# The factors of o: from a diagonal and a product to two transfers through memory

## The chip, the cores and the metric

The kernel runs on one core of a Trainium2 chip. The metric is the device time of one execution in microseconds. TensorE (PE in the profile) multiplies, VectorE (DVE), ScalarE (ACT) and GpSimd (POOL) work elementwise, SyncE (SP) issues most of the transfers.

## The reference, cut to what matters

A trunk of four layers over 528 tokens (16 meta tokens and 512 of the input) of 1024 channels: a mixer and a gated feed-forward block in each. The second mixer is a differential attention with 8 heads, and only it is touched:

```
s = q k^T * scale + bias                      # two score maps (c = 0, 1) per head
p = softmax(where(mask, s, -inf))
wts = p[:, :, 0] - lam * p[:, :, 1]
o = wts @ v                                   # 128 channels per head
o = rmsnorm(o, subln_g, 1e-5) * (1 - lam_init)
return o.reshape(B, L, 1024) @ w_o
```

The rmsnorm is over the 128 channels of one head, so each head has one factor 1/rms for each of the 528 tokens, and o is multiplied by it.

## The kernel before, in words

Each matrix product is done in three: every operand is split in a high part (rounded, type fp32r) and a low part (the rest), and hi x hi, lo x hi and hi x lo are summed. ACT makes high parts, DVE low parts.

In the attention o lies with the channels of a head on the 128 partitions and the tokens along the free dimension (`o_raw`, 128x528). The factor of a token must therefore be known on every partition. It comes about like this for head h:

- ACT copies the product of weights and v from PSUM to `o_raw` and squares it into `o_sq` (`copy_rows`, L1797 on). PE sums the squares over the partitions (`o_sums`, L1333), which puts token sums in five columns of 128 partitions, that is token j*128+p on partition p, column j, and the meta tokens in the fifth.
- DVE adds the epsilon and makes a first guess of the root (`guess_factors`, L2421 on, `rsqrt_seed`, L1987). It also tells POOL by the semaphore `o_guessed`.
- POOL refines the guess in two steps on 128x5 numbers (`row_factors`, L775 to L793), then scales the identity by each of the five columns into a diagonal `o_diag` of 128x528 (L796, L797), in the buffer that is called `square` in the profile.
- PE multiplies a matrix of ones by the diagonal (`spread_factors`, L1336 on, L1343 and L1344): each partition of PSUM banks 7 and 6 then holds all 528 factors.
- DVE multiplies `o_raw` by them and by the gain (`norm_rows`, L2440 and L2442) and drains. ACT makes the high part of o (`o_hi`, L1819) and DVE the low part (`o_lo`, L2450) in the next step, as operands of the output projection.

The work is a software pipeline whose order is written out by hand: each engine has its own `attention_step` (PE L1391 on, ACT L1821 on, DVE L2460 on), and step h does the q, k and v projection of head h, the scores, softmax and weights of head h-1, and the o of head h-2. Each engine runs its list in order, and semaphores tie them. Step 0 only projects, step 1 has no older head, steps 2 to 7 do all three, step 8 projects nothing (PE fills in with the output projection), and step 9 does the o of the last head, for which DVE and ACT build the diagonal by themselves. PE and DVE run steps 4 to 7 as a hardware loop, POOL ran its seven steps as one.

In one step of PE: half of the q projection between the transposes of the older head's last weights (L1309, L1385), weights times v (L1322), then score blocks 0 to 4 (L1298; block j is 128 queries against 16+(j+1)*128 keys, block 4 is the 16 meta queries) set between pieces of the k and v projection (L856), and turned weights. All score blocks use PSUM bank 4 and 5, so block j waits for the maxima of block j-1 (`scores_read`, L1298's `wait`). On DVE: for each block `row_maxima` (adds the bias, takes the maxima, L2378 and L2384), on ACT `exponentials` (L1780), on DVE `combine` (L2393 to L2398, the weights of a block), and `weights_lo` for the low part of the turned weights (L2412 to L2417). `norm_rows` of the older head stands on DVE between `row_maxima` of block 3 and `combine` of block 3, and `spread_factors` on PE in the third part of the v projection before score block 4. PSUM banks 6 and 7 are shared in turn by six users per step (last weights, v, sums, first weights, o's factors, third weights), which `turn_number` numbers: PE counts `turned`, and the readers count `turned_lo` when a bank may be overwritten.

Of the kernel before, what the change touches and what calls it, by code (L numbers as in the profile page):

```python
# [26 lines left out]
F32 = mybir.dt.float32  # L27
F32R = mybir.dt.float32r
I32 = mybir.dt.int32
ALU = mybir.AluOpType  # L30
ACT = mybir.ActivationFunctionType
ds = bass.ds

P = 128
# [146 lines left out]
class Memory:  # L181


    def __init__(self, nc, ctx):
# [93 lines left out]
        self.o_diag = self.square  # L278
        row_maxima = new("row_maxima", [P, 8])
# [41 lines left out]
class Semaphores:  # L321


    def __init__(self, sem):
# [64 lines left out]
        self.o_diagonal = sem("o_diagonal")  # L389
        self.o_rooted = sem("o_rooted")  # L390
# [66 lines left out]
def turn_number(h, what):  # L457

    if isinstance(h, int) and h == 1:
        return {"v": 0, "w01": 1, "w2": 2}[what]
    if isinstance(h, int) and h == HEADS + 1:
        return 6 * h - 9 + {"w3": 0, "sums": 1, "o": 2}[what]
    return h * 6 + ({"w3": 0, "v": 1, "sums": 2, "w01": 3, "o": 4, "w2": 5}[what] - 9)
# [27 lines left out]
def trunk(nc, a, out):  # L495
# [3 lines left out]
    with ctx:  # L499
# [5 lines left out]
        rel_once = nc.dram_tensor("rel_once", [HEADS, REL_PITCH], F32, kind="Internal").ap()  # L505
        bands_dram = nc.dram_tensor("bands_scratch", [P, 4, BANDS], F32, kind="Internal").ap()
# [187 lines left out]
        def _(pool):  # L694
# [80 lines left out]
            def row_factors(hd):  # L775
# [19 lines left out]
                for j in range(QT):  # L795
                    pool.tensor_scalar(m.o_diag[:, j * P:(j + 1) * P], m.ident[:, :], m.o_r[:, j:j + 1], None, ALU.mult)  # L796
                pool.tensor_scalar(m.o_diag[0:META, QT * P:TOK], m.ident[0:META, 0:META], m.o_r[0:META, QT:QT + 1],  # L797
                                   None, ALU.mult).then_inc(s.o_diagonal, 1)


            with pool.Fori(1, HEADS) as hd:
                pool.wait_ge(s.scores_read, hd * 5)
                pool.tensor_copy(m.bias_cur[:, :], m.bias[:, ds(hd * TOK, TOK)]).then_inc(s.bias_cur_ready, 1)
# [46 lines left out]
        def _(pe):  # L850
# [485 lines left out]
            def spread_factors(h):  # L1336

                pe.wait_ge(s.o_diagonal, h + 1)
                parts = ((0, DVE_TILES), (DVE_TILES, QT)) if isinstance(h, int) and h == HEADS - 1 else ((0, QT),)
                for n, (j0, j1) in enumerate(parts):  # L1340
# [46 lines left out]
            def attention_step(h, par, proj, mid, old):  # L1387
# [54 lines left out]
                if old:  # L1442
                    banks67_free(h, "o")
                    spread_factors(h2)
# [10 lines left out]
            def attention_end():  # L1455
# [17 lines left out]
                spread_factors(h2)  # L1473
# [493 lines left out]
        def _(dve):  # L1967
# [453 lines left out]
            def guess_factors(h, step):  # L2421
# [4 lines left out]
                if isinstance(h, int) and h == HEADS - 1:  # L2426
                    dve.wait_ge(s.o_diagonal, h)
# [9 lines left out]
            def norm_rows(h, step):  # L2437

                dve.wait_ge(s.turned, turn_number(step, "o") + 1)
# [249 lines left out]
```

## Time and profile before

| what | value |
|---|---|
| time, median of 3 runs | 2067.81 us (2063.7 to 2068.21) |
| profiled execution, span from the first to the last instruction | 2061.8 us |
| busy share of the span: PE, DVE, ACT, POOL | 98%, 76%, 43%, 11% |
| mean granted clock of TensorE | 0.987 |
| median of the runs over the profiled span | 6.0 us |

No time of its own is given for the profiled execution beside its span; what lies around the span is only known as the distance to the timed runs. A row of a timeline has the start in us from the beginning of the span, the duration in us, the engine, the line, the operation, what it writes and reads, the sizes, the count of merged instructions, and in brackets the idle time before and what ended it. Ends of matrix products are modelled, so their starts are the better numbers.

### The profile page before, as it was taken

How to read it: one execution, taken by the hardware profiler on the slowest of the kernel's cores; microseconds unless marked ns; L12 is line 12 of the kernel's file. 1: busy time of each engine (PE TensorE's matmuls, PEld its weight loads, DVE VectorE, ACT ScalarE, POOL GpSimd, SP SyncE). 2: the span in 40 equal slices, each digit the busy share in tenths (PEclk: the TensorE clock that was granted, in tenths of full speed). 3: DMA queues.
4: the chain of work that ended last, by engine and by line, in shares of the span. 5: the costliest groups of instructions: out<-in, count | busy, mean ns of one | idle time of the engine just before them, and what ended most of it. 6: DMA issues, size and time to landing. Idle time of an engine off the chain costs nothing.

```text
span 2061.8 us, 40642 instructions
## 1 busy us (share of the span) xinstructions
PE 2020.2 (98%) x16006; PEld 1950.4 (95%) x16006; DVE 1572.3 (76%) x2265; ACT 877.4 (43%) x1364; POOL 236.1 (11%) x340
## 2 busy tenths in 40 slices
PE   7999999999998999999999999999999999999998
PEld 7999999988887999999999999999999988999997
DVE  6797788766776579778877886687787867977794
ACT  6443334334444334333438764343343434433342
POOL 5000000412122400000041111100000061000000
PEclk9999999999998999999999998999999999999999
DMA  5423333331121132333336641233433422233332
GB/s 164 135 83 102 102 102 98 90 112 53 51 61 51 52 92 83 102 102 102 98 102 135 138 108 42 72 93 93 122 100 83 119 77 82 82 102 102 102 103 93
DMA packets 305226, 195.14 MB, mean 95 GB/s; under 512 B 7034, under 2 KB 297851, under 8 KB 304852
## 3 DMA queue, kind: packets, MB, share of 16 engines
q1 hardware_dynamic: 299932, 175.08, 29.6%
q0 software_dynamic: 3984, 14.08, 3.2%
q10 hardware_dynamic: 1192, 4.34, 0.5%
q8 instruction: 82, 1.34, 0.3%
q14 instruction: 36, 0.29, 0.0%
HBM read 179.44 MB, written 6.44 MB: 90 GB/s over the span
## 4 chain that ended last, share of the span: by engine, by line
PE 85%; DVE 6%; issue 3%; POOLq 1%; DVEq 1%; ACT 1%; DMA 1%; SPq 0%; POOL 0%; ACTq 0%
PE ps L856 42%; PE ps L1120 31%; PE ps L973 2%; PE ps L1231 2%; PE ps L914 1%; PE ps L1322 1%; PE ps L1298 1%; DVE w_lo L1974 1%; PE ps L957 1%; DVE w_lo L2213 1%; POOLq L750 1%; DVEq L2249 1%; DVEq L2218 1%; POOLq L747 1%; PE ps L883 1%
## 5 line engine op out<-in xcount | busy, mean ns | idle before, releaser
L1120 PE MATMUL ps<-t_lo,y_hi 128*128 128x264 f32 (+1 forms) x1008 | 285.7, 283 | 0.0
L1120 PE MATMUL ps<-t_lo,w_hi 128*128 128x264 f32 (+1 forms) x1008 | 285.7, 283 | 0.0
L1120 PE MATMUL ps<-t_hi,w_lo 128*128 128x264 f32 (+1 forms) x1008 | 285.5, 283 | 0.0
L1120 PE MATMUL ps<-t_hi,y_lo 128*128 128x264 f32 (+1 forms) x1008 | 285.3, 283 | 0.0
L1120 PE MATMUL ps<-t_hi,w_hi 128*128 128x264 f32 (+1 forms) x1008 | 285.1, 283 | 0.1
L1120 PE MATMUL ps<-t_hi,y_hi 128*128 128x264 f32 (+1 forms) x1008 | 284.8, 283 | 0.0
L1685 ACT ACTIVATE w_hi<-w_raw 128x1024 fp32r<-128x1024 f32 (+1 forms) x108 | 127.8, 1201 | 329.4 <-PE ps L856 193.8
L856 PE MATMUL ps<-hid_hi,w_hi 128*128 128x264 f32 (+1 forms) x1184 | 265.3, 296 | 1.6 <-DVE hid_lo L2269 1.6
L856 PE MATMUL ps<-hid_lo,w_hi 128*128 128x264 f32 (+1 forms) x1184 | 264.6, 296 | 0.0
L856 PE MATMUL ps<-hid_hi,w_lo 128*128 128x264 f32 (+1 forms) x1184 | 264.1, 295 | 0.0
L856 PE MATMUL ps<-y_hi,w_hi 128*128 128x264 f32 (+1 forms) x1088 | 244.1, 301 | 4.3 <-POOLq L827 2.3
L856 PE MATMUL ps<-y_lo,w_hi 128*128 128x264 f32 (+1 forms) x1088 | 234.6, 292 | 0.0
L856 PE MATMUL ps<-y_hi,w_lo 128*128 128x264 f32 (+1 forms) x1088 | 234.3, 292 | 0.0
L1685 ACT ACTIVATE y_hi<-w_raw 128x1024 fp32r<-128x1024 f32 (+1 forms) x108 | 125.8, 1197 | 166.2 <-DVE w_raw L2223 134.3
L856 PEld LDWEIGHTS ps<-hid_hi,w_hi 128*128 128x128 f32 x1184 | 187.2, 188 | 7.8 <-DVE hid_lo L2269 2.2
L856 PEld LDWEIGHTS ps<-hid_lo,w_hi 128*128 128x128 f32 x1184 | 187.6, 188 | 5.5
L856 PEld LDWEIGHTS ps<-hid_hi,w_lo 128*128 128x128 f32 x1184 | 187.4, 188 | 5.7
L1120 PEld LDWEIGHTS ps<-t_hi,w_hi 128*128 128x128 f32 x1008 | 189.8, 188 | 0.7 <-DVE h L2309 0.5
L1120 PEld LDWEIGHTS ps<-t_hi,y_hi 128*128 128x128 f32 x1008 | 189.8, 188 | 0.0
L1120 PEld LDWEIGHTS ps<-t_lo,w_hi 128*128 128x128 f32 x1008 | 189.5, 188 | 0.1
L1120 PEld LDWEIGHTS ps<-t_hi,w_lo 128*128 128x128 f32 x1008 | 189.5, 188 | 0.0
L1120 PEld LDWEIGHTS ps<-t_hi,y_lo 128*128 128x128 f32 x1008 | 189.5, 188 | 0.0
(317 smaller groups left out, 4410.9 us busy)
## 6 DMA issues: line engine op xcount, KB each, us to landing
w_raw<-in_ffn_w_gate SPq DMA_DIRECT2D x88, 512.0 KB, 5.0
w_raw<-in_ffn_w_up SPq DMA_DIRECT2D x88, 512.0 KB, 4.6
w_raw<-in_ffn_w_down SPq DMA_DIRECT2D x70, 512.0 KB, 4.3
w_raw<-in_ffn_w_down SPq DMA_DIRECT2D x24, 384.0 KB, 4.3
w_raw<-in_attn_w_qkv SPq DMA_DIRECT2D x16, 512.0 KB, 3.7
w_raw<-in_conv_w_in SPq DMA_DIRECT2D x16, 512.0 KB, 4.2
w_lo<-w_raw POOLq DMA_DIRECT2D x16, 512.0 KB, 5.4
w_raw<-in_attn_w_qkv SPq DMA_DIRECT2D x16, 256.0 KB, 2.9
```

The costliest lines, as they stand in the source:

```text
L747: pool.drain()
L750: pool.drain()
L856: mm = pe.matmul(ps[:, bank + hf, 0:half], w[:, slot, col:col + P], x(hf), start=begin and w is m.w_hi and n == 0, stop=end and w is m.w_lo)
L883: mm = pe.matmul(ps[:, 7, at:at + 1], blk(square, d, t, P), m.ones[:, 0:1], start=True, stop=True)
L914: mm = pe.matmul(out, y[:, at:at + rows], w[:, (t0 + g) % SLOTS, k * 256:(k + 1) * 256], start=k == 0 and n == 0, stop=k == 1 and n == 2)
L957: mm = pe.matmul(out[:, c0:c1], z, m.bands[0:TILE_ROWS[i], g, at:at + c1 - c0], start=i == 2 and n == 0, stop=i in (1, 4) and n == 1)
L973: mm = pe.matmul(ps[:, 4 * par + 2 + r, 0:cols_n], w[rows, par, :, :].rearrange("p t c -> p (t c)")[:, pairs_of_taps], u[rows, par, (j - r ...
L1120: mm = pe.matmul(ps[:, bank, 0:hw], w[:, at:at + P], b[:, t, k, 0:hw], start=k == 0 and n == 0, stop=k == 3 and n == 2)
L1231: mm = pe.matmul(bank, x, w, start=False, stop=k == LAST_F - 1 and n == 2)
L1298: mm = pe.matmul(ps[:, (4, proj_banks(par, 1))[part] + c, col:col + k1 - k0], q[rows, q0:q0 + P], k[rows, k0:k1], start=n == 0, stop=n == 2)
L1322: pe.matmul(ps[:, 4, q0:QT * P], v[0:rows, vi, :], w, start=n == 0 and x == 0, stop=n == QT and x == 2)
L1685: act.activation(hi[:, sub * SUB:(sub + n_sub) * SUB], src, ACT.Copy).then_inc(s.op_hi, 1)
```

## The change

For heads 0 to 6 the diagonal and the product with ones are gone. POOL, after its two steps of refinement, writes the 128x5 factors to a row of 640 numbers in memory, token by token, waits for that transfer, and reads the first 528 back to all 128 partitions by a second transfer, into the same buffer that held the diagonal (`o_factors`). Two semaphores, `factors_out` and `factors_in`, count them. The seven POOL steps are now written out instead of looped.

PE issues no spreading for these heads, and the numbering of banks 6 and 7 has five users per step. On DVE `norm_rows` waits for `factors_in`, reads the factors from SBUF, and stands later: behind `row_maxima` of block 4, the reading of v, and the low parts of q and k, before the low part of the third weights. For head 7 everything stays as it was.

```diff
@@ Memory
         self.o_diag = self.square
+        self.o_factors = self.square
@@ turn_number
     if isinstance(h, int) and h == HEADS + 1:
-        return 6 * h - 9 + {"w3": 0, "sums": 1, "o": 2}[what]
-    return h * 6 + ({"w3": 0, "v": 1, "sums": 2, "w01": 3, "o": 4, "w2": 5}[what] - 9)
+        return 5 * h - 7 + {"w3": 0, "sums": 1, "o": 2}[what]
+    return h * 5 + ({"w3": 0, "v": 1, "sums": 2, "w01": 3, "w2": 4}[what] - 7)
@@ POOL
+        factors_dram = nc.dram_tensor("o_factors_scratch", [(QT + 1) * P], F32, kind="Internal").ap()
...
-                for j in range(QT):
-                    pool.tensor_scalar(m.o_diag[:, j * P:(j + 1) * P], m.ident[:, :], m.o_r[:, j:j + 1], None, ALU.mult)
-                pool.tensor_scalar(m.o_diag[0:META, QT * P:TOK], m.ident[0:META, 0:META], m.o_r[0:META, QT:QT + 1],
-                                   None, ALU.mult).then_inc(s.o_diagonal, 1)
-            with pool.Fori(1, HEADS) as hd:
+                wait(pool, s.factors_in, hd * 16)
+                with nc.allow_non_contiguous_dma(reason="one factor a token"):
+                    pool.dma_start(factors_dram.rearrange("(j p) -> p j", p=P), m.o_r[:, :]).then_inc(s.factors_out, 16)
+                pool.wait_ge(s.factors_out, hd * 16 + 16)
+                pool.dma_start(m.o_factors[:, :],
+                               factors_dram[0:TOK].rearrange("(o n) -> o n", o=1).to_broadcast([P, TOK]))\
+                    .then_inc(s.factors_in, 16)
+            for hd in range(1, HEADS):
                 pool.wait_ge(s.scores_read, hd * 5)
-                pool.tensor_copy(m.bias_cur[:, :], m.bias[:, ds(hd * TOK, TOK)]).then_inc(s.bias_cur_ready, 1)
+                pool.tensor_copy(m.bias_cur[:, :], m.bias[:, hd * TOK:(hd + 1) * TOK]).then_inc(s.bias_cur_ready, 1)
                 row_factors(hd - 1)
@@ PE
-            def spread_factors(h):
-                pe.wait_ge(s.o_diagonal, h + 1)
-                parts = ((0, DVE_TILES), (DVE_TILES, QT)) if isinstance(h, int) and h == HEADS - 1 else ((0, QT),)
-                for n, (j0, j1) in enumerate(parts):
+            def spread_last_factors():
+                pe.wait_ge(s.o_diagonal, 1)
+                for n, (j0, j1) in enumerate(((0, DVE_TILES), (DVE_TILES, QT))):
...
                 fill(2, 2, 5)
-                if old:
-                    banks67_free(h, "o")
-                    spread_factors(h2)
                 if mid:
                     score(h1, par, 4)
@@ DVE
             def norm_rows(h, step):
-                dve.wait_ge(s.turned, turn_number(step, "o") + 1)
-                dve.scalar_tensor_tensor(out=m.o_raw[:, META:], in0=ps[:, 7, :], scalar=m.sub_gain[:, 0:1],
+                last = isinstance(h, int) and h == HEADS - 1
+                if last:
+                    dve.wait_ge(s.turned, turn_number(step, "o") + 1)
+                    tokens, meta = ps[:, 7, :], ps[:, 6, 0:META]
+                else:
+                    dve.wait_ge(s.factors_in, h * 16 + 16)
+                    tokens, meta = m.o_factors[:, 0:SEQ], m.o_factors[:, SEQ:TOK]
+                dve.scalar_tensor_tensor(out=m.o_raw[:, META:], in0=tokens, scalar=m.sub_gain[:, 0:1],
...
                     row_maxima(h1, par, 3)
-                if old and mid:
-                    norm_rows(h2, h)
                 if mid:
                     combine(h1, 3)
                     row_maxima(h1, par, 4)
...
                         dve.tensor_tensor(lo[:, :], x[:, :], hi[:, :].bitcast(F32), ALU.subtract)\
                            .then_inc(s.qk_ready, 1)
+                if old and mid:
+                    norm_rows(h2, h)
                 if mid:
                     weights_lo(h, "w2", 2, 2)
                     combine(h1, 4)
```

## Rows read from the trace of the kernel before

**Rows 1.** The page: busy time and share of the engines, and the chain by engine.
```profile
PE 2020.2 (98%) x16006; PEld 1950.4 (95%) x16006; DVE 1572.3 (76%) x2265; ACT 877.4 (43%) x1364; POOL 236.1 (11%) x340
...
PE 85%; DVE 6%; issue 3%; POOLq 1%; DVEq 1%; ACT 1%; DMA 1%; SPq 0%; POOL 0%; ACTq 0%
```

**Rows 2.** Timeline of PE in step 4 (start, duration, engine, line, operation, tiles, count).
```profile
533.96 0.45 PE L1298 MATMUL ps<-k_hi,q_hi 64*128 64x400 f32 x2
...
541.60 1.02 PE L1343 MATMUL ps<-square,ones 128*128 128x512 f32 x2
...
542.87 0.28 PE L1298 MATMUL ps<-k_hi,q_hi 64*128 64x16 f32 x2
...
549.17 0.65 PE L1309 MATMUL ps<-ident,weights 128*128 128x128 f32 x4
...
549.88 0.33 PE L1385 MATMUL ps<-ident,weights_meta 128*128 128x128 f32 x1
...
553.88 0.49 PE L1322 MATMUL ps<-wtm_hi,v_hi 16*128 16x512 f32 x1
```

**Rows 3.** Timeline of DVE in step 4.
```profile
542.59 0.17 DVE L2384 TENSOR_SCALAR row_maxima<-row_maxima 128x2 f32<-128x2 f32 x1
542.98 0.75 DVE L2440 SCALAR_TENSOR_TENSOR o_raw<-ps,lam_s,o_raw 128x512 f32<-128x512 f32 x1 [0.22 <-PE ps L1344]
543.65 0.23 DVE L2442 SCALAR_TENSOR_TENSOR o_raw<-ps,lam_s,o_raw 128x16 f32<-128x16 f32 x1
544.38 0.16 DVE L2393 RECIPROCAL row_maxima<-row_sums 128x1 f32<-128x1 f32 x1 [0.50 <-ACT scores L1780]
...
548.38 0.55 DVE L2412 TENSOR_TENSOR wt_lo<-ps,wt_hi 128x384 fp32r<-128x384 f32 x1
...
549.60 0.22 DVE L2398 SCALAR_TENSOR_TENSOR weights_meta<-scores,row_maxima 16x16 f32<-16x16 f32 x1
```

**Rows 4.** Timeline of PE in step 1, which has no older head.
```profile
443.65 0.45 PE L1298 MATMUL ps<-k_hi,q_hi 64*128 64x400 f32 x2
...
452.42 0.28 PE L1298 MATMUL ps<-k_hi,q_hi 64*128 64x16 f32 x2 [0.98 <-DVE row_maxima L2384]
...
458.81 0.65 PE L1309 MATMUL ps<-ident,weights 128*128 128x128 f32 x4 [0.15 <-DVE wtm_lo L2417]
```

**Rows 5.** Timeline of DVE in step 1.
```profile
453.98 0.16 DVE L2393 RECIPROCAL row_maxima<-row_sums 128x1 f32<-128x1 f32 x1 [1.61 <-ACT scores L1780]
```

**Rows 6.** The last refining multiplication, grouped (durations min/median/max in ns).
```profile
L793 POOL TENSOR_TENSOR o_r<-o_t,o_r x14: 195/198/1149, 474.5 to 657.3; 128x5 f32<-128x5 f32 x14
```

**Rows 7.** Timeline of POOL, steps 4 and 8.
```profile
537.54 2.35 POOL L796 TENSOR_SCALAR square<-ident,o_r 128x128 f32<-128x128 f32 x4 [0.17 <-issue]
...
657.67 2.34 POOL L796 TENSOR_SCALAR square<-ident,o_r 128x128 f32<-128x128 f32 x4 [0.17 <-issue]
```

**Rows 8.** Transfers: tiles, issuing queue, count, size of each, median us to landing.
```profile
w_raw<-in_attn_w_qkv SPq DMA_DIRECT2D x16, 256.0 KB, 2.9
...
bias<-rel_scratch POOLq DMA_DIRECT2D x1, 2112.0 KB, 10.0
...
cv_sum<-cv POOLq DMA_DIRECT2D x7, 264.0 KB, 6.7
```

**Rows 9.** Timeline of PE in step 8.
```profile
660.45 2.05 PE L1343 MATMUL ps<-square,ones 128*128 128x512 f32 x2 [2.19 <-POOL square L797]
...
669.48 0.60 PE L1309 MATMUL ps<-ident,weights 128*128 128x128 f32 x4
```

**Rows 10.** Timeline of DVE in step 8.
```profile
662.86 0.17 DVE L2384 TENSOR_SCALAR row_maxima<-row_maxima 128x2 f32<-128x2 f32 x1
...
666.61 0.54 DVE L2412 TENSOR_TENSOR wt_lo<-ps,wt_hi 128x384 fp32r<-128x384 f32 x1
...
668.01 0.22 DVE L2398 SCALAR_TENSOR_TENSOR weights_meta<-scores,row_maxima 16x16 f32<-16x16 f32 x1
```

**Rows 11.** Stretches: PE, PEld, DVE, ACT, POOL busy (instructions), granted clock, DMA share, GB/s.
```profile
658.00:662.00 4.00, 1.81 (x6) 0.50 (x2) 2.96 (x11) 0.62 (x2) 2.31 (x5) 0.50 0.00 0
```

More of the change, by code:

```diff
@@ L389, in __init__ @@
         self.o_diagonal = sem("o_diagonal")
+        self.factors_out = sem("factors_out")
+        self.factors_in = sem("factors_in")
         self.o_rooted = sem("o_rooted")
@@ L1472, in attention_end @@
                 banks67_free(HEADS + 1, "o")
-                spread_factors(h2)
+                spread_last_factors()
                 attn_out(2, HEADS - 2)
@@ L2425, in guess_factors @@
                                          in1=m.row_eps[:, :], op0=ALU.mult, op1=ALU.add).then_inc(s.turned_lo, 1)
-                if isinstance(h, int) and h == HEADS - 1:
-                    dve.wait_ge(s.o_diagonal, h)
                 rsqrt_seed(m.o_x[:, :], m.o_r[:, :]).then_inc(s.o_guessed, 1)
@@ L2437, in norm_rows @@
             def norm_rows(h, step):
-                dve.wait_ge(s.turned, turn_number(step, "o") + 1)
-                dve.scalar_tensor_tensor(out=m.o_raw[:, META:], in0=ps[:, 7, :], scalar=m.sub_gain[:, 0:1],
+                last = isinstance(h, int) and h == HEADS - 1
[6 more added lines that the diff above has]
+                dve.scalar_tensor_tensor(out=m.o_raw[:, META:], in0=tokens, scalar=m.sub_gain[:, 0:1],
                                          in1=m.o_raw[:, META:], op0=ALU.mult, op1=ALU.mult)
-                dve.scalar_tensor_tensor(out=m.o_raw[:, 0:META], in0=ps[:, 6, 0:META], scalar=m.sub_gain[:, 0:1],
-                                         in1=m.o_raw[:, 0:META], op0=ALU.mult, op1=ALU.mult)\
-                   .then_inc(s.turned_lo, 1)
+                e = dve.scalar_tensor_tensor(out=m.o_raw[:, 0:META], in0=meta, scalar=m.sub_gain[:, 0:1],
+                                             in1=m.o_raw[:, 0:META], op0=ALU.mult, op1=ALU.mult)
+                if last:
+                    e.then_inc(s.turned_lo, 1)
                 dve.drain().then_inc(s.o_normed, 1)
```

## The prediction

> **What bounds the kernel now.** First the busy table: PE is busy 98% of the span, DVE 76%, and the chain that ended last is put down to PE for 85% [rows 1]. By these two alone, a PE instruction that goes is time won. But they are averages, and the change touches only one stretch, the attention. So next I read one step of its loop on PE and DVE, and ask of each PE instruction there which wait would end last. I take the step that holds the spreading product at 541.60. Five more look like it (spreading at 481.26, 511.27, 571.84, 602.48 and 632.75); the seventh product stands in the last step, which has no projection.
>
> What the reader is to see on PE [rows 2]: spreading from 541.60 to the fifth score block (64x16) at 542.87; transposes of the last weights at 549.17 and 549.88; weights times v at 553.88. On DVE [rows 3]: the fourth block's maxima are there at 542.59+0.17 = 542.76; the factors are multiplied in from 542.98 to 543.65+0.23 = 543.88; then DVE idles 0.50 us until ACT has the exponentials of that block. From 544.38 on it is nearly without a pause up to the meta rows' weights, 549.60+0.22 = 549.82, and PE transposes exactly those at 549.88. It runs on to the first maxima of the next scores, which PE's product at 553.88 waits for. So PE is full, but at 549.88 DVE is right behind it: the cover is 0.06 us.
>
> **Part 1: the product goes from PE.** It held PE for 542.87-541.60 = 1.27 us. But the next instruction, the fifth score block, writes the banks that the fourth's maxima are read from, and so waits for 542.76. With the spreading gone PE waits there for DVE. The trace holds a control: the loop's first step with scores has neither spreading nor factors, and there PE waited 0.98 us for the row maxima before this very block [rows 4]. From its third score block to the transposes of the last weights that step took 458.81-443.65 = 15.16 us; the step with spreading took 549.17-533.96 = 15.21 [rows 2, 4]. I value the removed product at nothing. Bounds: a gain of 1.2 us per step if no wait takes its place, and 0; a loss is excluded but for the clock (a rival below).
>
> **Part 2: the multiplication moves on DVE.** It leaves the place where DVE waits for ACT anyway: in the control step, which has no multiplication, that wait is 1.61 us instead of 0.50 [rows 3, 5], so what follows is not earlier. It goes behind q_lo and k_lo, into the stretch where DVE has no pause. Behind it stand the low part of the third weights and the meta weights (PE asks for both, at 549.17 and 549.88), the low part of a weight tile, o_lo, the low part of the fourth weights, and the first maxima (PE asks at 553.88). Its size is 543.65-542.98 = 0.67, plus 0.23: 0.90 us [rows 3]. The drain behind it adds a little, the cover of 0.06 takes a little off; I leave both out. PE is dense from there to the next step's third score block, so DVE's lateness is handed on whole and nothing gives it back. Six steps: 6 x 0.90 = 5.4 us. Bounds per step: 0, if something before it has slack that I don't see, and 1.1 with a drain and a wait of 0.1 each way; a gain is excluded, since nothing in front of it gets shorter. The factors are now read from SBUF, not PSUM; that could move its size a few hundredths. ACT's rounding of o follows it; ACT is busy 43% [rows 1] and has time to move it in.
>
> **Part 3: POOL and the two transfers.** POOL's scalings (four of 128x128 in 2.35 us from 537.54 [rows 7], and a small one) go; POOL is idle after them, so nothing by itself. The transfers start instead of them at 537.54, and DVE comes to the multiplication at 548.38 [rows 3]: a cover of 10.8 us. The first writes 640 runs of 4 bytes, the second reads a row of 2112 bytes for each of 128 partitions. The trace shows neither. Nearest rows [rows 8]: 256 KB loaded by SP land in 2.9 us; 264 KB that POOL accumulates in 6.7; POOL's 2112 KB in 1024 runs in 10.0. The second transfer has the size of the first two, the queue of the one and the plain copy of the other: the middle, 4.8. The first has next to no bytes but 640 runs: above 2.9, and far under 10.0, whose bytes alone are eight times 256 KB; I take 4.7, nearer to 2.9. Sum 9.5, there 1.3 us before DVE asks: hidden, at nothing. Bounds: 2 x 2.9 = 5.8 and 10.0+6.7 = 16.7. Between the two POOL waits; behind it in its queue is the copy of the next head's bias, which starts only at 546.66: hidden too. SP's load of a weight tile issued at 537.48 shares the DMA engines; the row of 2.9 us is of such loads and holds them.
>
> One kind of delay is shown: the same small multiplication on POOL took 0.20 us as a median and 1.15 at most [rows 6], so something holds POOL up for 0.95. One such hold per transfer adds 1.9 us, and 9.5 becomes 11.4: late by 0.6. The Trainium skill's page SBUF — State Buffer (SBUF: two separate sides) speaks against the change: a GpSimd-issued transfer has its descriptors written over a port that it shares with VectorE, and can stand while VectorE runs in a 2-port mode, 620 ns becoming 3100. By it (an estimate from the page) two transfers are up to 5 us later, 14.5, and the kernel 6 x 3.7 + 4.7 = 27 us slower still. The row shows the hold, not one of that length.
>
> **Part 4: the last step.** PE's wait of 2.19 us for POOL and the spreading behind it go [rows 9]. But the fifth score block again waits for the maxima, 662.86+0.17 = 663.03 [rows 10], and the spreading had ended about there (two products from 660.45, 2.05 us, and two small ones): nothing gained. DVE comes to the multiplication at 666.61. What PE asks for at 669.48 was ready at 668.01+0.22 = 668.23 [rows 9, 10], so 0.90 fits; the transfers, from 657.67 [rows 7], have 8.9 us and the 0.3 that is left, 9.2. The clock is another matter: the two products of 128x512 took 2.05 us here and 1.02 in the loop [rows 2, 9], and from 658 to 662 the granted clock is 0.50, the lower level of 1.2 GHz, after PE had paused [rows 11]. Without them PE does nothing from 660.45-2.19 = 658.3 to 663.0. If the clock comes back later by the 2.6 us of work that is gone, PE gets 1.3 less done. Bounds 0 and 1.3; I take the middle, 0.7.
>
> **Sum.** 5.4 + 0.7 = 6.1 us slower, against the profiled span of 2061.8: 2067.9. The runs shown (2063.7 to 2068.21) have a median of 2067.81, 6.0 above that span with what lies around it; kept, it gives **2073.9 us**.
>
> **Rivals.**
> Late factors. One mechanism: the pair of transfers takes over 10.8 us, DVE stands, and all that part 2 names stands behind it. From there each microsecond costs one in each of six steps, in the last from 9.2 on. Two of POOL's 6.7 are 13.4: 6 x 2.6 + 4.2 = 20 more, 2094; at 12.3: 6 x 1.5 + 3.1 = 12 more, 2086. For it: POOL's rows and the hold. Against: both transfers are small. Chance 0.27.
>
> PE is the bound; this is the other side. If the fifth block's wait is short and DVE has a microsecond of cover at 549.88, the chain's own count holds: 6 x 1.2 = 7.2 saved, in the last step up to 663.0-658.3 = 4.7: 12 faster, 2056. For it: 98% and 85%. Against: the control's 0.98 us, and the cover of 0.06. Chance 0.10.
>
> Absorbed: DVE's move meets slack, PE gains nothing, or a part of each cancels: 2064 to 2071. Chance 0.12.
>
> Clock: two waits of about a microsecond in each step bring the granted clock down; 4 us at half speed cost 2 per step, 12 more, 2086. Against: the control waited 0.98 at full clock. Chance 0.01.
>
> The forecast keeps 0.50; its own range is 2071 to 2078.
>
> **How the numbers follow.** About 0.2%, 4.1 us, is what a measurement here can tell from no change: slower means above 2071.9, faster under 2063.7. Slower: 0.45 of the forecast, 0.28 of late factors and clock, together 0.73. Same: 0.05 of the forecast, 0.12 absorbed, 0.17. Faster: 0.10. The range goes down to 2065, which leaves out the PE rival, and up to 2087, which leaves out factors later than about 12.4 us, another 0.10.
>
> **What would show it.** In the trace after: PE idle some 1.2 us between the fourth and fifth score block, released by the row maxima; a second wait of PE, of about 1 us, before the transposes of the last weights or the meta weights; from the third score block to those transposes 16.1 us instead of 15.2; DVE's wait for exponentials before the fourth weights over 1 us; no idle time of DVE before the multiplication. If that distance stays at 15.3 or less, part 2 is wrong. If DVE idles before the multiplication, part 3 is, and the length of that wait times six is what the first rival adds.

## The result, and the profile after

The kernel after takes **2108.95 us** (median of 4 runs, 2107.69 to 2113.84), the kernel before 2068.01 on the same chip; the ratio is **1.0222**, 95% interval [1.021, 1.0233]. The prediction of 2073.9 and its range up to 2087 are missed by far; only the direction is right. The profiled execution after spans 2105.8 us, 44.0 more than the 2061.8 of before. (Of all executions below, one of e10's six took 3928.44 us; what disturbed it isn't known, and no ratio uses it.)

The page after, busy table, chain by engine and the two new transfers (the rows that answer to [rows 1] and [rows 8]):

```profile
PE 2025.9 (96%) x15978; PEld 1960.1 (93%) x15978; DVE 1574.3 (75%) x2265; ACT 879.9 (42%) x1364; POOL 227.5 (11%) x319
...
PE 78%; issue 9%; DMA 4%; POOLq 4%; DVE 3%; DVEq 1%; ACT 1%; POOL 0%; SPq 0%; ACTq 0%
...
square<-o_factors_scratch POOLq DMA_DIRECT2D x7, 264.0 KB, 4.4
...
o_factors_scratch<-o_r POOLq DMA_DIRECT2D x7, 2.5 KB, 8.9
```

The last number of a transfer's row is the median time from issue to landing. The smallest transfer of the kernel, 2.5 KB, takes 8.9 us, twice as long as the 264 KB behind it.

PE in step 4, from the third score block to that of the next step (answers to [rows 2]; in brackets the idle time before, and who ended it):

```profile
546.45 0.45 PE L1305 MATMUL ps<-k_hi,q_hi 64*128 64x400 f32 x2
...
555.31 0.28 PE L1305 MATMUL ps<-k_hi,q_hi 64*128 64x16 f32 x2 [1.05 <-DVE row_maxima L2387]
...
567.13 1.12 PE L1316 MATMUL ps<-ident,weights 128*128 128x128 f32 x4 [5.54 <-DVE wtm_lo L2420]
568.25 0.42 PE L1391 MATMUL ps<-ident,weights_meta 128*128 128x128 f32 x1
...
584.16 0.45 PE L1305 MATMUL ps<-k_hi,q_hi 64*128 64x400 f32 x2
```

The removed product has become a wait of 1.05 us for the row maxima, as in the control step of [rows 4]. Then there is a second wait, 5.54 us, before the last weights' transposes. From the third block to them it is now 567.13-546.45 = 20.68 us where it was 15.21. The prediction had 16.1.

DVE and POOL in that step (answers to [rows 3] and [rows 7]):

```profile
556.88 0.16 DVE L2396 RECIPROCAL row_maxima<-row_sums 128x1 f32<-128x1 f32 x1 [1.62 <-ACT scores L1783]
...
560.16 0.69 DVE L2519 TENSOR_TENSOR k_lo<-k,k_hi 128x528 fp32r<-128x528 f32 x1
565.25 0.75 DVE L2447 SCALAR_TENSOR_TENSOR o_raw<-square,lam_s,o_raw 128x512 f32<-128x512 f32 x1 [4.40 <-DMA square<-o_factors_scratch]
565.92 0.23 DVE L2449 SCALAR_TENSOR_TENSOR o_raw<-square,lam_s,o_raw 128x16 f32<-128x16 f32 x1
```
```profile
550.36 0.20 POOL L797 TENSOR_TENSOR o_r<-o_t,o_r 128x5 f32<-128x5 f32 x1
551.13 0.91 POOL L801 DMA_DIRECT2D o_factors_scratch<-o_r  x1 [0.57 <-issue]
560.73 0.59 POOL L803 DMA_DIRECT2D square<-o_factors_scratch  x1 [8.69 <-DMA o_factors_scratch<-o_r]
```

POOL has its factors at 550.56. It takes 0.57 us to get to the first transfer, waits until 560.73 for it, and DVE is released at 565.25: 14.7 us, where DVE was ready after 560.85-550.56 = 10.3. DVE stands for 4.40 us, and the third and meta weights stand behind it. In all it waits 25.2 us over seven steps (us in total, times, longest):

```profile
DVE o_raw L2447 <- DMA square<-o_factors_scratch: 25.2, 7, 5.9
```

What the transfer does in that time is seen in the first two stretches, of 2 us each (PE, PEld, DVE, ACT, POOL busy, granted clock, DMA share, GB/s); the last two rows, of 4 us, show the clock behind PE's long pause, the one before them 40 us of the loop:

```profile
556.00:558.00 2.00, 2.00 (x18) 2.00 (x18) 0.95 (x3) 1.92 (x6) 0.00 (x0) 1.00 0.00 0
558.00:560.00 2.00, 2.00 (x19) 2.00 (x19) 1.73 (x9) 1.23 (x6) 0.00 (x0) 1.00 0.00 0
...
540.00:580.00 40.00, 33.41 (x250) 30.46 (x247) 22.85 (x75) 16.47 (x45) 5.42 (x13) 0.91 0.18 47
...
566.00:570.00 4.00, 2.87 (x14) 2.41 (x15) 3.62 (x11) 1.93 (x5) 0.00 (x0) 0.50 0.00 0
570.00:574.00 4.00, 4.00 (x25) 3.86 (x24) 2.98 (x14) 1.05 (x5) 0.00 (x0) 0.72 0.50 140
```

From 556 to 560 the DMA engines show no busy time at all, though the transfer issued at 551.13 has not landed: it is waiting, not moving. The records of the DMA engines say the same in finer steps: the last of its sixteen packets has ended at 553.65, and its sixteen completions come one by one from 554.54 to 560.43. And behind the pause of 5.54 us the granted clock is at its lower level (0.50, 1.2 GHz), just where PE has work again. From the transposes to the next step's third score block it took 584.16-567.13 = 17.03 us; before it took 564.20-549.17 = 15.03, and e1 below, in the new order and at full clock, takes 15.02. So the clock costs this step 2.0 us more. The whole step lasts 584.16-546.45 = 37.71 us instead of 30.24.

The 44 us lie in the attention alone. Two marks serve for all kernels: the third score block of step 2 (before 473.62, after 472.96) and PE's wait of 1.52 us for o_lo at the end of the last head (before 686.85, after 730.61):

```profile
730.61 0.51 PE L863 MATMUL ps<-o_hi,w_hi 128*128 128x264 f32 x2 [1.52 <-DVE o_lo L2458]
```

Between them lie 213.2 us before and 257.6 after, 44.4 more. I call this distance the stretch. Six steps of the loop take 38.7 of it (third block of step 2 to that of step 8, at 652.62 before and 690.70 after), the last step 5.7. The 38.7 divide in DVE's waits for factors, 25.2 - 5.9 (the last step's) = 19.3; the moved multiplication, some 5.8 (measured below, in e1); and a remainder of 13.6. Step by step against e1, the way from the last weights' transposes to the next third block is 0.6 to 2.8 us longer, 11.3 in the six steps: this is the clock. Of the 2.3 left, 2.0 are DVE instructions that lasted longer beside POOL's copy of the next bias (shown with e3).

### The profile page after: what moved, and what is told of

Read it like the earlier page. It is cut to its first block, busy times and chain, and to the rows that moved or that the text cites. A ratio compares the mean times of both kernels' runs of the same rounds, so it can differ in the third digit from the quotient of the medians.

```text
span 2105.8 us, 40518 instructions
## 1 busy us (share of the span) xinstructions
PE 2025.9 (96%) x15978; PEld 1960.1 (93%) x15978; DVE 1574.3 (75%) x2265; ACT 879.9 (42%) x1364; POOL 227.5 (11%) x319
## 4 chain that ended last, share of the span: by engine, by line
PE 78%; issue 9%; DMA 4%; POOLq 4%; DVE 3%; DVEq 1%; ACT 1%; POOL 0%; SPq 0%; ACTq 0%
PE ps L863 37%; PE ps L1127 33%; DMA o_factors_scratch<-o_r 3%; PE ps L980 2%; PE ps L1238 2%; POOLq L754 1%; PE ps L921 1%; POOLq L751 1%; PE ps L964 1%; PE ps L890 0%; POOLq L796 0%; DVE w_lo L2216 0%; DVEq L2252 0%; PE ps L897 0%; PE ps L877 0%
```

## Experiments

For each kernel the stretch is given against the 213.2 us of before; it is free of the few microseconds by which executions differ ahead of the attention. The kernel before, run again beside the experiments, took 2063.3 to 2064.7 us as a median, less than the 2068.01 above; so kernels are compared by their ratios, and each stretch is that of one execution.

### The parts one by one

**e1_no_transfers** keeps the moved multiplication and takes the transfers out:
```diff
-                [POOL's two transfers and its waits for them]
+                pool.engine_nop().then_inc(s.factors_in, 1)
...
-                    dve.wait_ge(s.factors_in, h * 16 + 16)
+                    dve.wait_ge(s.factors_in, h + 1)
-                    tokens, meta = m.o_factors[:, 0:SEQ], m.o_factors[:, SEQ:TOK]
+                    tokens, meta = m.rstd[:, 0:SEQ], m.rstd[:, SEQ:TOK]
```


> Left out: both transfers; the multiplication takes the row of rstd (already in SBUF) in place of the factors, so o is scaled wrongly; DVE waits only for POOL's last refining step. All else as in the changed kernel. Theory (late transfers cost 25 us of waiting, the falling clock behind them about 12, the moved multiplication 0.97 us in each of six steps, the removed product nothing): 2074 us (2072 to 2077), granted clock back at full in steps 2 to 7, third score block to the last weights' transposes 16.1 us. Rival, PE is the bound and its product was worth 1.2 us a step: 2056 to 2062. Rival, the move itself brings the clock down and costs most: above 2085.

**e2_old_place** is e1 with `norm_rows` back between the maxima of block 3 and the weights of block 3:
```diff
                     row_maxima(h1, par, 3)
+                if old and mid:
+                    norm_rows(h2, h)
                 if mid:
                     combine(h1, 3)
```


> As e1 (no transfers, the multiplication takes rstd), but the multiplication stands at its old place, before the weights of the fourth block. What is left of the change is that PE has no spreading product. Theory: the fifth score block waits about 1.0 us for the row maxima instead, so 2068 us as before, within 2, third score block to last transposes 15.2 us. Rival, PE is the bound: 7 x 1.2 and 2 to 4 more in the last step gained, 2056 to 2060.

Measured: e1 2072.19 us, ratio 1.0048 [1.0032, 1.0065], stretch +5.6. e2 2064.18, ratio 1.0005 [0.9995, 1.0015], stretch -1.2. PE in step 4 of e1, then of e2:

```profile
539.38 0.45 PE L1299 MATMUL ps<-k_hi,q_hi 64*128 64x400 f32 x2
...
555.57 0.66 PE L1310 MATMUL ps<-ident,weights 128*128 128x128 f32 x4 [1.08 <-DVE wtm_lo L2414]
...
570.59 0.45 PE L1299 MATMUL ps<-k_hi,q_hi 64*128 64x400 f32 x2
```
```profile
536.53 0.45 PE L1299 MATMUL ps<-k_hi,q_hi 64*128 64x400 f32 x2
...
545.37 0.28 PE L1299 MATMUL ps<-k_hi,q_hi 64*128 64x16 f32 x2 [1.04 <-DVE row_maxima L2381]
...
551.64 0.66 PE L1310 MATMUL ps<-ident,weights 128*128 128x128 f32 x4
```

e2 takes 15.11 us for the distance that took 15.21 before: the product is gone, a wait of 1.04 us stands in its place, and nothing is won. e1 takes 16.19, 0.98 more than before: the multiplication in its new place costs its full length. Both are what the prediction's parts 1 and 2 say. With the transfers away the granted clock is 0.985 again (before: 0.987), and the loss is the 5.6 us of the stretch, where the forecast's sum was 6.1; by its ratio the kernel would have taken 2078 us beside the 2068 of the result, at the edge of the forecast's own range. All the rest of the loss hangs on the transfers.

**e3_unread** does both transfers as the kernel after, but the multiplication doesn't wait for them (DVE only waits, before it overwrites the factors, until the first transfer of the head before has read them):
```diff
-                    dve.wait_ge(s.factors_in, h * 16 + 16)
-                    tokens, meta = m.o_factors[:, 0:SEQ], m.o_factors[:, SEQ:TOK]
+                    dve.wait_ge(s.o_diagonal, h + 1)
+                    tokens, meta = m.rstd[:, 0:SEQ], m.rstd[:, SEQ:TOK]
...
```


> The changed kernel with both transfers running as they do, but nothing on DVE waits for the second: the multiplication takes rstd at its new place. Theory: the transfers cost only by being late, so the same as e1 within 2 us, 2074. Rival, contention: they slow DVE, the weight loads or POOL's copies, 5 us or more above e1.

Measured: 2075.17 us, ratio 1.007 [1.0053, 1.0087]. Its interval overlaps that of e1, though its median is 3.0 us higher, between the theory's 2 and the rival's 5. So the presence of the transfers is worth 0 to some 5 us, and it is the wait for them that costs most. Its stretch is +10.9, 5.3 more than e1's, and the trace shows where they come from. First, POOL copies the next head's bias behind the second transfer, and so later than in e1. In e1 this copy ran beside DVE's reading of v from PSUM, which took 0.69 us as before; in e3 it falls in each of the six steps on a DVE instruction whose inputs are in SBUF, and that instruction lasts 0.50 to 0.83 us longer than its like, 3.8 us in all:

```profile
552.55 1.52 DVE L2522 TENSOR_TENSOR k_lo<-k,k_hi 128x528 fp32r<-128x528 f32 x1
```
```profile
552.86 0.64 POOL L811 COPY bias_cur<-bias 128x528 f32<-128x528 f32 x1
```

In e1 `k_lo` took 0.70 us. Second, two steps took 33.4 and 33.1 us among others of 31.5 to 32.0. In the first of the two, PE paused 1.87 us (e1: 1.08), and the clock fell behind it:

```profile
554.00:558.00 4.00, 2.13 (x15) 1.76 (x16) 3.66 (x11) 1.71 (x5) 0.00 (x0) 0.93 0.33 68
558.00:562.00 4.00, 4.00 (x24) 3.86 (x22) 3.17 (x14) 1.26 (x5) 0.00 (x0) 0.65 0.47 131
```

The length of the pause doesn't decide it by itself: in e3 pauses of 1.87 and 1.61 us before these transposes were followed by the lower level, those of 1.57, 1.69, 1.69 and 1.73 us were not; e1 and e4 stayed at 1.00 in the loop with 0.9 to 1.4 us. In the kernel after all six (4.2 to 5.5 us) were followed by it. The clock is thus a second part of the cost, behind the wait.

### What makes the first transfer long

**e4_runs20** writes the five factors of a partition side by side, 128 runs of 20 bytes. The tokens' order in the row is then another, so that o is scaled by other tokens' factors.
```diff
-    pool.dma_start(factors_dram.rearrange("(j p) -> p j", p=P), m.o_r[:, :])
+    pool.dma_start(factors_dram.rearrange("(p j) -> p j", p=P), m.o_r[:, :])
```


> The changed kernel, with the scratch row laid out partition by partition, so that the first transfer writes 128 runs of 20 bytes instead of 640 of 4; the row then comes back in another order, so o is scaled by the wrong tokens' factors. Theory A, the number of runs makes the first transfer long (8.9 us): it falls to 4 to 5 us, DVE waits little or nothing, the clock stays up, 2075 to 2080. Rival B, it is the fixed cost of a transfer issued by POOL that writes to memory: it stays above 8 us and the kernel above 2103.

**e5_runs_doubled** writes 128x10 numbers, 1280 runs of 4 bytes:
```diff
-    pool.dma_start(factors_dram.rearrange("(j p) -> p j", p=P), m.o_r[:, :])
+    pool.dma_start(factors_dram.rearrange("(j p) -> p j", p=P), m.o_r2[:, :])    # 128 x 10
```


> The changed kernel, but the first transfer writes 1280 runs of 4 bytes (the five factors and five ones of each partition) instead of 640; the second reads the same first 528 numbers. Theory, the cost is by the run: from 3.0 us with 128 runs and 8.9 with 640 it is 11.5 ns per run, so 16.3 us now, 7.4 more in each of seven steps: the changed kernel plus 52, and more where PE, idle for longer, gets its clock back later: 2160 to 2180. Rival, a step between 20-byte and 4-byte runs and not their number: first transfer under 10.5 us and under 2120.

Measured: e4 2070.59 us, ratio 1.0039 [1.0025, 1.0054], stretch +5.9, no wait of DVE for factors. e5 2113.19 (2 runs), ratio 1.0233 [1.0213, 1.0254], stretch +48.3. POOL's waits for the first transfer, e4 and e5 (us in total, times, longest; after: 58.6, 7, 9.2):

```profile
POOL square L803 <- DMA o_factors_scratch<-o_r: 19.6, 7, 3.7
```
```profile
POOL square L805 <- DMA o_factors_scratch<-o_r: 66.1, 7, 10.2
```

e4's theory A held (3.0 us, where it said 4 to 5): take the short runs away and the remaining cost is the multiplication's. e5 missed by far. I had divided the 5.9 us between e4 and after by the 512 runs between them, 11.5 ns each, and expected 2160 to 2180. Doubling the runs added 1.1 us per transfer, under 2 ns a run, as its rival had it (under 10.5 us for the transfer, under 2120 for the kernel). The number of runs is not what most of the 8.9 us is made of. In the next three kernels the second transfer reads a row of an input instead of the scratch row, so the factors are other numbers.

**e11_one_column** sends 128 factors only, **e12_spread64** all 640 with 64 bytes from each to the next, **e14_near** all 640, 8 bytes apart, partition by partition. **e6_sp_queue** leaves the transfers as they are and lets SP issue them.
```diff
@@ e11_one_column
+    pool.dma_start(factors_dram[0:P].rearrange("(p j) -> p j", j=1), m.o_r[:, 0:1])
@@ e12_spread64
+    pool.dma_start(factors_dram.rearrange("(j p n) -> p j n", p=P, n=16)[:, :, 0:1], ...m.o_r...)
@@ e14_near
+    pool.dma_start(factors_dram.rearrange("(p j n) -> p j n", p=P, n=2)[:, :, 0:1], ...m.o_r...)
@@ e6_sp_queue
+                sp.wait_ge(s.o_diagonal, hd + 1)
...
+                    sp.dma_start(factors_dram.rearrange("(j p) -> p j", p=P), m.o_r[:, :]).then_inc(s.factors_out, 16)
...
```


> The first transfer sends only the first column of o_r: 128 runs of 4 bytes to 128 neighbouring words, in place of 640; the second transfer reads a row of an input of the same size (left out: the true factors, so o is scaled by other numbers). The kernel after took 8.9 us for 640 runs of 4 bytes, 128 runs of 20 bytes took 3.0 us, 1280 runs of 4 bytes about 10. Theory A, the number of runs up to some hundreds sets it: the first transfer takes about 3 us here, as with 20-byte runs, and the time is near 2070. Theory B, each run under some size makes a slow write whatever their number: it stays at 8 to 9 us, and the time near 2105. Theory C, 4-byte writes that are neighbours in memory wait for each other: between the two, 4 to 7 us, since 128 of them are still neighbours.

> The first transfer sends all 640 factors as 4-byte runs, but each to its own word 64 bytes from the next, so no two share 64 bytes of memory; the second transfer reads a row of an input of the same size (left out: the true factors). Theory A (number of runs): 8.9 us as in the kernel after, time near 2108. Theory B (each short run is a slow write): the same 8.9. Theory C (neighbouring short writes wait for each other): 3 to 4.5 us, and the time falls to 2070 to 2080.

> The first transfer sends all 640 factors as 4-byte runs, a partition's five 8 bytes apart and the partitions one after the other, so that the runs of one partition lie near each other as in the 20-byte version, but don't join; the second transfer reads a row of an input of the same size (left out: the true factors). Theory A and B: 8.9 us, time near 2108. Theory C: no better than 8.9, since neighbours still share 64 bytes. A fourth, D, the order in memory (in the kernel after a partition's five words lie 512 bytes apart): 3 to 4 us and a time near 2070.

> The kernel after with both transfers issued by SP instead of POOL, the first still 640 runs of 4 bytes. If the queue of POOL (its issue of 0.91 us, its descriptors made by the engine) makes the first transfer long, it falls from 8.9 us to 3 to 5 us, DVE's waits for factors (25.2 us over 7) go to under 5, and the time to 2072 to 2078. If the short runs themselves make it, it stays at 8 us or more; POOL's issues go (0.91 and 0.59 us, beside nothing on the path), SP's loads of weights around them come later by up to 13 us, and the time stays at 2100 to 2112.

The first transfer's row in e11, e12, e14, e6 and, last, e4:

```profile
o_factors_scratch<-o_r POOLq DMA_DIRECT2D x7, 0.5 KB, 7.6
```
```profile
o_factors_scratch<-o_r POOLq DMA_DIRECT2D x7, 2.5 KB, 3.2
```
```profile
o_factors_scratch<-o_r POOLq DMA_DIRECT2D x7, 2.5 KB, 5.0
```
```profile
o_factors_scratch<-o_r SPq DMA_DIRECT2D x7, 2.5 KB, 8.8
```
```profile
o_factors_scratch<-o_r POOLq DMA_DIRECT2D x7, 2.5 KB, 3.0
```

| kernel | runs | apart | separate writes in 64 bytes | first transfer | stretch |
|---|---|---|---|---|---|
| e12 | 640 of 4 bytes | 64 bytes | 1 | 3.2 us | +6.0 |
| e4 | 128 of 20 bytes | none | 3.2 | 3.0 | +5.9 |
| e14 | 640 of 4 bytes | 8 bytes | 8 | 5.0 | +6.4 |
| e11 | 128 of 4 bytes | none | 16 | 7.6 | +25.5 |
| after | 640 of 4 bytes | none | 16 | 8.9 | +44.4 |
| e6, SP's queue | 640 of 4 bytes | none | 16 | 8.8 | +39.6 |

The single executions took 2089.09 us (e11), 2067.29 (e12) and 2071.5 (e14), beside 2064.68 of before; e6 2104.57, ratio 1.0194 [1.0175, 1.0213]. 640 separate writes are fast if they lie apart, 128 are slow if they are neighbours: theory C. The count (A) and the shortness by itself (B) fall with e12, the queue and the engine that issues fall with e6. The order in memory (D) falls too: e12 keeps the order of after and is fast, e11 has one word per partition, in order, and is slow. C's numbers were not exact: for e11 it had said 4 to 7 and 7.6 came out, so that the count adds a little (7.6, 8.9, and about 10 in e5); for e14 it had said no better than 8.9, and 5.0 came out. The time rises with how many separate writes share a small piece of memory. The whole difference lies behind the packets: in step 4 they have ended 1.6 us after POOL's issue in after and in e12 alike (553.65-552.04, 543.98-542.42), but the last completion comes another 6.8 us later in after and 0.5 us later in e12 (over the seven steps 5.6 to 6.8, 0.5 to 0.7, and in e14 2.2 to 2.6). What in the memory or in the DMA engines makes neighbours wait isn't shown, nor the size of the piece: 8 and 64 bytes were the only distances tried. The Trainium skill says on its page DMA: Bandwidth & Descriptors (Anatomy of one DMA — SWDGE (gpsimd) path) that the semaphore comes only when the last byte is confirmed in the target memory, which is most of its fixed 2 us. The trace agrees in kind: after the engines' busy time is over the transfer stays open for microseconds.

### Is there a version that pays

**e9_runs20_right** is e4 made complete: the row is read as it lies, and DVE picks each token's factor five words apart.
```diff
+    pool.dma_start(factors_dram.rearrange("(p j) -> p j", p=P), m.o_r[:, :])
+                    f = m.o_factors[:, :].rearrange("q (p j) -> q j p", j=QT + 1)
+                    tokens, meta = f[:, 0:QT, :], f[:, QT, 0:META]
```


> Complete: the changed kernel with the scratch row partition by partition (128 runs of 20 bytes), all 640 numbers read back, and DVE reading them with a stride of five. Theory: first transfer 3.0 us, second 3.6 to 4.0, no wait; only the moved multiplication is left: 0.35% to 0.6% above before, as with e1 and e4. Rival: a strided read slows DVE's multiplication (0.75 us) and adds up to 0.7 us per step, 1% above before.

Measured: 2073.26 us, ratio 1.0040 [1.0026, 1.0055], stretch +10.7 (in the slowest of its five executions, 2079.08 us). The strided multiplication takes 1145 ns where e4's takes 740, groups of six in steps 2 to 7:

```profile
L2449 DVE SCALAR_TENSOR_TENSOR o_raw<-bias,lam_s,o_raw 128x512 f32<-128x512 f32 x6 | 6.9, 1145 | 0.0
```
```profile
L2447 DVE SCALAR_TENSOR_TENSOR o_raw<-square,lam_s,o_raw 128x512 f32<-128x512 f32 x6 | 4.4, 740 | 0.0
```

6 x 0.405 = 2.4 us of the 4.8 between the two stretches; in two steps, of 33.0 us among others of 31.4 to 32.0, the clock fell behind pauses of 1.52 us. So the change with its transfers mended is still 0.4% slower than before, for the multiplication stands where DVE has no pause.

**e7_late** leaves the transfers long and gives them time: o waits in a block of the bias that is no longer needed, and the multiplication comes a step later, between the first weights and the reading of q.
```diff
                     combine(h1, 0)
+                if mid and older:
+                    norm_rows(h - 3, h)
                 if proj:
...
-                if old and mid:
-                    norm_rows(h2, h)
                 if mid:
                     weights_lo(h, "w2", 2, 2)
```


> Complete. The transfers stay as in the change (640 runs), but the multiplication, and the rounding of o behind it, move on by one more step, to where DVE and ACT wait for the product of weights and v; o stands in the blocks of the bias that are used up, and the loops of DVE and ACT over the heads are written out. The factors then have 19 us instead of 10.8. Theory: no wait for factors (they need 14.7), no clock fall in steps 2 to 7, DVE's run before the meta weights as long as before the change: within 3 us of the kernel before, on either side; it can't be clearly faster, since DVE still has 0.06 us of cover at the meta weights. Rival, transfers through memory cost by themselves: 5 us or more above before.

**e8_late_reordered** is e7 with a new order that closes PE's gap before the fifth score block: it comes after all fill steps, the first one two fill steps later, and ACT and DVE split the third weights ahead of the projections' reads, DVE a weight tile ahead of the fourth block's weights.
```diff
@@ PE
+                fill(0, 4, 6, (0, 2))
                 if mid:
                     pe.wait_ge(s.qk_ready, h1 * 2 + 2)
                     score(h1, par, 0)
-                fill(0, 4, 8, (0, 2), (0, 3), (0, 4))
+                fill(0, 6, 8, (0, 3), (0, 4))
...
-                fill(2, 2, 5)
+                fill(2, 2, 8)
                 if mid:
                     score(h1, par, 4)
-                fill(2, 5, 8)
@@ DVE
                     row_maxima(h1, par, 4)
+                    weights_lo(h, "w2", 2, 2)
                 if proj:
                     read_projection(h, par, 2, m.v, 1.0)
```


> Complete: e7, and the order written anew so that DVE's chain is shorter than PE's: DVE splits the fourth weight tile while it waits for the exponentials, takes the third weights' low part and the meta weights ahead of the low parts of q and k; PE puts the fifth score block behind all of the v projection and the first score block two products later; ACT rounds the third weights before q and k. Theory: with the waits at the fifth score block (1.05 us) and before the last weights (0.3) gone, the 1.2 us of the removed product come out in each of six steps: 6 to 9 us below before. Rival, DVE's waits only move to the next instruction: within 2 us of before.

**e13_before_reordered** takes over the order of e8 in the kernel before, its product left in. **e10_late_runs20_reordered** is e8 with the transfers of e9.

> The kernel before, with its diagonals and spreading product as they were, and only the new order of e8_late_reordered: two fill steps ahead of the first score block, the fifth score block after all fill steps, the third weights' split ahead of the projections' reads. e8 measured 0.9945 of before. Theory A, the gain of e8 is the order's alone (it empties PE's seven waits of about 1 us for the row maxima ahead of the fifth score block, 12.2 us to 5.6 us in all): 2056 to 2060, ratio 0.996 to 0.998. Theory B, the order is only worth something once the spreading product is gone, for with it the product stood in that gap and DVE reads its result later: 2063 to 2070, ratio 0.999 or above. Theory C, the removed product was itself worth its PE time once nothing waits (0.44 us at the bound of 1.2 us a step): e13 lies 3 to 8 us above e8.

> e8_late_reordered with the first transfer in 128 runs of 20 bytes, DVE reading the factors five words apart. Theory A: in e8 the multiplication comes a step later, so that the 14 us of the transfers are hidden already; taking 5 to 6 us off them gives nothing: ratio 0.993 to 0.997, DVE's waits for factors (1.0 us over 2) go to none. Theory B: the multiplication's strided read costs DVE time that shows: 2 to 4 us above e8, ratio 0.996 to 0.998. Theory C: the long transfers delay something else in e8 (POOL's next bias copy): 2 us or more below e8.

| kernel | us | ratio to before, 95% | stretch |
|---|---|---|---|
| e7_late | 2062.61 | 0.9989 [0.9978, 1.0000] | -2.0 |
| e13_before_reordered | 2065.27 | 1.0007 [0.9998, 1.0016] | +0.9 |
| e8_late_reordered | **2054.63** | 0.9945 [0.9924, 0.9967] | -7.0 |
| e10_late_runs20_reordered | 2055.95 | 0.9955 [0.9942, 0.9968] | -6.9 |

PE's waits for the row maxima in the attention, e7 and then e8:

```profile
PE ps L1306 <- DVE row_maxima L2387: 12.2, 9, 4.8
```
```profile
PE ps L1306 <- DVE row_maxima L2388: 5.6, 2, 4.8
```

One step of PE in e13, from the third score block to the next step's, and the same in e8:

```profile
533.58 0.45 PE L1298 MATMUL ps<-k_hi,q_hi 64*128 64x400 f32 x2
...
541.23 1.02 PE L1343 MATMUL ps<-square,ones 128*128 128x512 f32 x2
...
544.89 0.28 PE L1298 MATMUL ps<-k_hi,q_hi 64*128 64x16 f32 x2
...
563.83 0.45 PE L1298 MATMUL ps<-k_hi,q_hi 64*128 64x400 f32 x2
```
```profile
532.70 0.45 PE L1306 MATMUL ps<-k_hi,q_hi 64*128 64x400 f32 x2
...
542.62 0.28 PE L1306 MATMUL ps<-k_hi,q_hi 64*128 64x16 f32 x2
...
561.33 0.45 PE L1306 MATMUL ps<-k_hi,q_hi 64*128 64x400 f32 x2
```

The step takes 30.25 us in e13, as before (30.24), and 28.63 in e8; PE has no pause over 0.2 us in either. What is gone is the product's length, 1.27 us by [rows 2], and a little around it. e13 came out as its theory B said (2063 to 2070), and not as A, which gave the whole gain to the order; C was right that the product is worth its time, but e13 lies 10.6 us above e8 and not 3 to 8. Removing the product alone gives nothing (e2), for PE then waits for the maxima; the new order alone gives nothing (e13), for where the product stood PE had no wait to close. The control stands in e13 itself: step 1 has no product, and there it takes 28.61 us (before 29.97), as e8's does (28.60). Step 1 has no multiplication by factors either, though, and e8 differs from e13 in that too, since it multiplies elsewhere; the new order with the product out and the multiplication at its old place wasn't run. Together the two edits save 179.0-171.6 = 7.4 us in the six steps and 1.4 in step 1, 8.8 of the 9.8 between the medians of before and e8. e10 does not differ from e8, for a pair of transfers of some 14 us costs next to nothing where it is hidden (e8's DVE waits 1.0 us for factors, in two steps).

## Why the prediction was wrong, point by point

- **Part 1, the product is worth nothing:** right. Fifth block 1.05 us late by the maxima (forecast: some 1.2), e2 at -1.2 us of stretch. Its bound of 1.2 us a step was real as well: e8 cashes it, with another order.
- **Part 2, the moved multiplication, 0.90 a step:** right in place and mechanism, a little small in size. e1 took 0.98 more in the step shown, and its six steps 184.76 us against 179.00: +5.8 where 5.4 was forecast. The wait for exponentials is 1.62, as said.
- **Part 3, the transfers hidden:** this is the step that failed. Of its terms the second transfer (4.8) measured 4.4; POOL took 0.57 us to get to the first, and no long hold shows at either issue (0.91 and 0.59 us). The first, **4.7 us, measured 8.9**. I took it "nearer to 2.9" because it has next to no bytes, and gave its 640 runs a little. The error was to ask for the price of a run, when what sets most of it is neither count nor bytes but that the runs are neighbours. None of the rows shown of before is a write of short runs to neighbouring words, so they could not show it. The total, 14.7 us, does lie inside my bounds of 5.8 to 16.7, but the range did not: its upper end let in factors only up to 12.4 us and left the rest, at 0.10, outside. That a term bounded so widely was taken at one row's side is what made the range too narrow.
- **The rule weighed there:** the Trainium skill's page SBUF — State Buffer (SBUF: two separate sides) gave 14.5 us by the estimate and 27 us on the time (with the last step's cover of 9.2 its second term is 5.3 and not 4.7, so 27.5). The sum was nearly met, the cause was not: with SP issuing, the first transfer still took 8.8 us (e6), and with 20-byte runs on POOL's queue it took 3.0 (e4). The traces don't bear the rule out as the cause here.
- **Part 4, the last step:** its cover of 9.2 us failed with part 3, and DVE stood 5.92 us there (710.69 in the timeline of DVE). The place was read rightly: in e2 the fifth block of that step comes 10.46 us after the third, exactly as before (663.08-652.62), so removing PE's 2.19 us of waiting for POOL and the product behind it gave nothing. The clock's 0.7 did not show: the last step takes 34.2 us before, 34.1 in e1 and 33.8 in e2.
- **Late factors (0.27):** this rival came true, with its place and its mechanism; at 14.7 us its own formula gives 6 x 3.9 + 5.5 = 29 more, about 2103. DVE's waits were somewhat shorter (25.2), for over the seven steps the pair took 13.6 to 15.0 us, and in three of them DVE came later itself; and the clock, 11.3 us in the six steps, was not in it.
- **Clock (0.01):** given as a case of its own, with two waits of about one microsecond and 4 us at half speed, for which no row was named. Such waits left the clock up in e1, e4 and e12; in e14 it fell in one of six steps. But it is no case of its own: PE's pauses behind the late factors, 4.2 to 5.5 us, were followed by the lower level in every step (0.91 in each 40 us of the loop) and cost 0.6 to 2.8 us each beyond themselves. I should have added it to that rival.
- **What would show it:** DVE idling before the multiplication was named as the sign that part 3 is wrong, and it was. That the wait times six is what the rival adds held only for the first part of the cost, without the clock.

## What to carry to other kernels

Don't write a column of 4-byte numbers to neighbouring words of memory by one transfer if somebody waits for it: let each partition write its numbers side by side, or read the row back so late, one step later here, that its time is hidden. An instruction removed from the busiest engine is won only when what then waits in its place is moved too; measure removal, reorder, and both. A pause that a late transfer makes on PE has to be priced with the clock behind it, not as the pause alone.

## What the runs showed of the hardware

- 640 four-byte writes landed in 3.2 us when 64 bytes apart, in 5.0 at 8 bytes, in 8.9 as neighbours; 128 neighbours took 7.6, 128 runs of 20 bytes 3.0. Issued by SP the 640 neighbours took 8.8. In step 4 the packets had ended 1.6 us after the issue in the fast and the slow case alike; the last completion came 6.8 us behind them with neighbours (after), 0.5 us with 64 bytes between (e12).
- PE pauses of 4.2 to 5.5 us before the last transposes (after) were each followed by a granted clock of 0.50; behind one of 5.54 us the step lost 2.0 us more. Shorter ones went both ways: 1.61 and 1.87 us with it, 1.69 and 1.73 without (e3).
- A DVE instruction with both inputs in SBUF lasted 0.50 to 0.83 us longer when POOL's copy of 0.64 us ran beside it (e3); the one that reads PSUM did not (0.69, e1).
- DVE's 128x512 multiplication took 740 ns from SBUF (e4), 1145 with one operand read five words apart (e9).
